# A gate table from fp32r products with high and low gates, its one-hots from two digits, and six Gelus behind the gates' exponent

## The reference

```python
def chunk_fn(xc):
    q = (xc @ w_query).reshape(C, PEER_HEADS, 2, PEER_HALF)
    sc = jnp.einsum('thpd,hpnd->thpn', q, sub_keys)
    top_s, top_i = lax.top_k(sc, 16)
    ...
    best_s, best_pos = lax.top_k(cand_s, 16)
    experts = jnp.take_along_axis(cand_i, best_pos, axis=-1)   # i1 * 128 + i2
    gates = jax.nn.softmax(best_s, axis=-1)
    u, vv = expert_down[experts], expert_up[experts]
    act = gelu(jnp.einsum('cd,chkd->chk', xc, u))
    return jnp.einsum('chk,chkd->cd', gates * act, vv)
```

## Time and profile before

| | |
|---|---|
| median of 3 runs | 1761.45 us (1759.91 to 1761.52) |
| profiled execution, its own time | 1758.45 us |
| its span, first to last instruction | 1756.3 us |
| mean granted TensorE clock | 0.963 of full |
| TensorE busy | 1594.7 us |
| VectorE busy | 1078.8 us |
| ScalarE busy | 712.9 us |

### The profile page before, as it was taken

The page is one execution under the profiler, slowest core; times in us unless marked ns, Lnnn a source line. Parts: engine busy times, 40 slices in busy tenths (PEclk is TensorE's granted clock), DMA queues, the critical chain, the costliest instruction groups (busy, mean ns, idle before and its releaser), DMA issues. The chain is left out here.

```text
span 1756.3 us, 29202 instructions
## 1 busy us (share of the span) xinstructions
PE 1594.7 (91%) x9001; PEld 1408.5 (80%) x9001; DVE 1078.8 (61%) x2744; ACT 712.9 (41%) x1526; POOL 5.1 (0%) x11
## 2 busy tenths in 40 slices
PE   2997699999998999999999999699999998778897
PEld 1664488879997888999999999589999997568785
DVE  2577457948996776666666666555455554257664
ACT  1333211113323444444444444365555554345552
POOL 0000000000000000000000000000000000000000
PEclk9998799999999999999999999799999999689998
DMA  6310133432224555555555555465555552065510
GB/s 257 145 37 1 44 131 119 151 131 85 91 91 168 192 193 191 185 184 191 190 185 186 183 188 191 173 205 144 147 147 147 138 129 53 1 206 158 160 30 24
DMA packets 151066, 244.50 MB, mean 139 GB/s; under 512 B 24144, under 2 KB 79952, under 8 KB 149968
## 3 DMA queue, kind: packets, MB, share of 16 engines
q1 hardware_dynamic: 150640, 243.51, 43.9%
q10 hardware_dynamic: 352, 0.07, 0.0%
HBM read 242.33 MB, written 1.20 MB: 139 GB/s over the span
## 5 line engine op out<-in xcount | busy, mean ns | idle before, releaser
L184 PE MATMUL experts_acc<-experts_uh,experts_wh 128*128 128x512 f32 x512 | 201.5, 394 | 5.6 <-DVE experts_ul L1546 5.6
L185 PE MATMUL experts_acc<-experts_ul,experts_wh 128*128 128x512 f32 x512 | 201.1, 393 | 0.0
L186 PE MATMUL experts_acc<-experts_uh,experts_wl 128*128 128x512 f32 x512 | 200.1, 391 | 0.0
L1099 PE MATMUL plain_u<-ffn_h,down_raw 128*128 128x256 f32 x832 | 192.2, 382 | 0.4 <-PEq L1184 0.4
L1519 ACT ACTIVATE experts_uh<-ffn_h 128x512 fp32r<-128x512 f32 x256 | 147.2, 623 | 83.7 <-PE experts_acc L186 79.0
L186 PE MATMUL projection<-hT_high,down_low 128*128 128x256 f32 x608 | 172.1, 283 | 0.0
L185 PE MATMUL projection<-hT_low,down_high 128*128 128x256 f32 x608 | 172.0, 283 | 0.0
L184 PE MATMUL projection<-hT_high,down_high 128*128 128x256 f32 x608 | 171.7, 282 | 0.0
L1099 PEld LDWEIGHTS plain_u<-ffn_h,down_raw 128*128 128x128 f32 x832 | 154.1, 192 | 19.5 <-issue 1.1
L1546 DVE TENSOR_TENSOR experts_ul<-ffn_h,experts_uh 128x512 fp32r<-128x512 f32 x256 | 164.8, 684 | 3.0 <-ACT experts_uh L1519 2.8
L184 PE MATMUL mix_a_pj<-mix_a_wh,hT_high 128*128 128x384 f32 x384 | 137.5, 358 | 18.2 <-DVE mix_a_wl L546 18.2
(11 more groups left out here) (270 smaller groups left out, 3083.5 us busy)
## 6 DMA issues: line engine op xcount, KB each, us to landing
down_raw<-in_downT SPq DMA_DIRECT2D x256, 256.0 KB, 3.5
ffn_h<-in_up SPq DMA_DIRECT2D x256, 256.0 KB, 2.8
mix_a_w_raw<-in_wa SPq DMA_DIRECT2D x48, 768.0 KB, 6.2
block_w_raw<-in_w SPq DMA_DIRECT2D x16, 768.0 KB, 6.3
mix_b_w_raw<-in_wb SPq DMA_DIRECT2D x16, 768.0 KB, 6.6
route_raw<-in_route SPq DMA_DIRECT2D x16, 576.0 KB, 3.8
bias_a<-bias_rows SPq DMA_DIRECT2D x16, 576.0 KB, 7.5
wo<-in_wo SPq DMA_DIRECT2D x2, 2048.0 KB, 10.3
```

The lines of the kernel that those rows point to most:

```text
L184: pe.matmul(out, lhs[0], rhs[0], start=start, stop=False, skip_group_check=True)
L185: pe.matmul(out, lhs[0], rhs[1], start=False, stop=False, skip_group_check=True)
L186: return pe.matmul(out, lhs[1], rhs[0], start=False, stop=stop, skip_group_check=True)
L1099: mm = pe.matmul(self.u[b][:, 0:SEQ], self.raw[b][:, k, :], self.h[:, k, :], start=k == 0, stop=k == KD - 1, skip_group_check=True)
```

## The change

1. EARLY goes from 28 to 24 and LATE from 24 to 28: four chunks are projected in `spread_phase` instead of `route_phase`. There TensorE takes 8 + 3 steps ahead of the first group (LEAD) and 3.375 per group afterwards, and a chunk is joined two groups behind its last step instead of one.
2. ScalarE computes the gates' exponent behind the 18th Gelu, and the last six Gelus after it.
3. VectorE finds the second index first. It splits the first index into a coarse digit (0 to 15) and a fine one (0 to 7), in four more operations on 128x256. Four arrays are turned and copied instead of three.
4. `a1` has a high part and a low part, both fp32r, and TensorE makes two fp32r products per token instead of one f32 product. The one-hots of the digits are made for eight groups at a time (`digits`), the coarse ones times the high gate; `a1h` is one product of the two per group on VectorE. ScalarE makes `a1l` from `a1h` by four activations per group whose scale is the ratio of low to high gate (`a1_low`), and does this for group g+1 before it evicts group g.

```diff
-EARLY = 28
-LATE = 24
+EARLY = 24
+LATE = 28
+BEFORE_GATE = 18
+LEAD = 8
+FINE = 8
...
-            for n, src in enumerate((index[0], index[1], gate)):
+            for n, src in enumerate((index[1], coarse, fine, gate)):
...
-            over_chunks(act, 0, EARLY, lambda n, b: plain.gelu(act, n, b, early[:, n, :]))
+            def early_gelu(n, b):
+                plain.gelu(act, n, b, early[:, n, :])
+            over_chunks(act, 0, BEFORE_GATE, early_gelu)
             act.wait_ge(shifted_ready, 1)
             act.activation(gate[:], shifted[:], ACT.Exp).then_inc(gate_exp, 1)
+            over_chunks(act, BEFORE_GATE, EARLY, early_gelu)
...
-            for half in range(2):
+            for half in (1, 0):
...
+            dve.tensor_scalar(eighth[:], index[0][:], 1.0 / FINE, -0.5 + 0.5 / FINE, ALU.mult, ALU.add)
+            dve.drain()
+            dve.tensor_scalar(eighth[:], eighth[:], WHOLE, None, ALU.add)
+            dve.drain()
+            dve.tensor_scalar(coarse[:], eighth[:], -WHOLE, None, ALU.add).then_inc(cols_ready, 1)
+            dve.drain()
+            dve.scalar_tensor_tensor(fine[:], coarse[:], -float(FINE), index[0][:], ALU.mult, ALU.add).then_inc(cols_ready, 1)
...
+    def steps_by(g):
+        return LEAD + (STEPS - LEAD) * (g + 1) // GROUPS if g >= 0 else 0
+    joins = [min(next(g for g in range(GROUPS) if steps_by(g) >= (n + 1) * KD) + 2, GROUPS) for n in range(LATE)]
...
+            def digits(n):
+                t = slice(n * BATCH * Q, (n + 1) * BATCH * Q)
+                for of, digit, base in ((coarse_of, "coarse", COARSE), (fine_of, "fine", FINE)):
+                    dve.tensor_tensor(of[:], iota[:, 0:base].unsqueeze(1).broadcast_to([P, BATCH * Q, base]),
+                                      slotT[digit][:, t].unsqueeze(2).broadcast_to([P, BATCH * Q, base]), ALU.is_equal)
+                dve.drain()
+                dve.tensor_tensor(coarse_of[:], coarse_of[:],
+                                  gate_h[:, t].bitcast(F32).unsqueeze(2).broadcast_to([P, BATCH * Q, COARSE]), ALU.mult)
+                dve.drain()
...
             def onehots(g):
                 b = g % 2
+                if g % BATCH == 0:
+                    digits(g // BATCH)
+                q = slice(g % BATCH * Q, g % BATCH * Q + Q)
                 wait(dve, g_ready, g - 1)
-                for q in range(Q):
-                    col = slice(g * Q + q, g * Q + q + 1)
-                    last = dve.tensor_scalar(a1[b][:, q, :], iota[:], slotT["i1"][:, col], slotT["gate"][:, col],
-                                             ALU.is_equal, ALU.mult)
-                last.then_inc(a1_ready, 1)
+                dve.tensor_tensor(a1h[b][:].rearrange("p q (h l) -> p q h l", l=FINE),
+                                  coarse_of[:, q].unsqueeze(3).broadcast_to([P, Q, COARSE, FINE]),
+                                  fine_of[:, q].unsqueeze(2).broadcast_to([P, Q, COARSE, FINE]), ALU.mult).then_inc(a1_ready, 1)
...
+            dve.tensor_copy(gate_h[:], slotT["gate"][:])
+            dve.drain()
+            dve.tensor_tensor(ratio[:], slotT["gate"][:], gate_h[:].bitcast(F32), ALU.subtract)
+            dve.tensor_scalar(floor[:], gate_h[:].bitcast(F32), TINY, None, ALU.max)
+            dve.drain()
+            dve.reciprocal(floor[:], floor[:])
+            dve.drain()
+            dve.tensor_tensor(ratio[:], ratio[:], floor[:], ALU.mult).then_inc(ratio_ready, 1)
...
                 for q in range(Q):
-                    mm = pe.matmul(gp[g % BANKS][:, q, :], a2[g % 2][:, q, :], a1[g % 2][:, q, :], start=True, stop=True)
+                    if q == 0:
+                        pe.wait_ge(a1l_ready, g + 1)
+                    pe.matmul(gp[g % BANKS][:, q, :], a2[g % 2][:, q, :], a1h[g % 2][:, q, :], start=True, stop=False,
+                              skip_group_check=True)
+                    mm = pe.matmul(gp[g % BANKS][:, q, :], a2[g % 2][:, q, :], a1l[g % 2][:, q, :], start=False, stop=True,
+                                   skip_group_check=True)
...
+            def a1_low(g):
+                act.wait_ge(a1_ready, g + 1)
+                wait(act, g_ready, g - 1)
+                for q in range(Q):
+                    last = act.activation(a1l[g % 2][:, q, :], a1h[g % 2][:, q, :].bitcast(F32), ACT.Copy,
+                                          scale=ratio[:, g * Q + q:g * Q + q + 1])
+                last.then_inc(a1l_ready, 1)
+            act.wait_ge(ratio_ready, 1)
+            a1_low(0)
             for g in range(GROUPS):
+                if g + 1 < GROUPS:
+                    a1_low(g + 1)
                 act.wait_ge(g_ready, g + 1)
```

More of the change, by code:

```diff
@@ L55 @@
 SKEW = 384
+WHOLE = 1.5 * float(1 << 23)
+TINY = 1e-30
 ROOT_SEED = float(0x5F3759DF - 0x00400000 - (1 << 30))
@@ L1210, in route_phase @@
         index = [sb(f"index{h}", [P, NT, SLOTS]) for h in range(2)]
+        eighth, coarse, fine = [sb(n, [P, NT, SLOTS]) for n in ("eighth", "coarse", "fine")]
         qp = [ps(f"qp{b}", [P, 512]) for b in range(2)]
@@ L1313, in _ @@
             dve.drain()
-            dve.tensor_scalar(part[:], pos[:], 4, None, ALU.logical_shift_right).then_inc(shifted_ready, 1)
+            dve.tensor_scalar(part[:], pos[:], TOPK - 1, None, ALU.bitwise_and).then_inc(shifted_ready, 1)
             dve.drain()
-            for half in range(2):
-                if half == 1:
-                    dve.tensor_scalar(part[:], pos[:], TOPK - 1, None, ALU.bitwise_and)
+            for half in (1, 0):
+                if half == 0:
+                    dve.tensor_scalar(part[:], pos[:], 4, None, ALU.logical_shift_right)
                     dve.drain()
@@ L1331, in _ @@
                     last = dve.tensor_reduce(index[half][:, t, :], picked[:], AX.X, ALU.add)
-                    if t == NT - 1:
+                    if half == 1 and t == NT - 1:
                         last.then_inc(cols_ready, 1)
                     dve.drain()
+            dve.tensor_scalar(eighth[:], index[0][:], 1.0 / FINE, -0.5 + 0.5 / FINE, ALU.mult, ALU.add)
[5 more added lines that the diff above has]
+            dve.scalar_tensor_tensor(fine[:], coarse[:], -float(FINE), index[0][:], ALU.mult, ALU.add).then_inc(cols_ready, 1)
             dve.wait_ge(gate_exp, 1)
@@ L1354, in spread_phase @@
     BANKS = 4
-    joins = [min(((n + 1) * KD * GROUPS + STEPS - 1) // STEPS + 1, GROUPS) for n in range(LATE)]
+    COARSE = P // FINE
+    BATCH = 8
+    def steps_by(g):
+        return LEAD + (STEPS - LEAD) * (g + 1) // GROUPS if g >= 0 else 0
+    joins = [min(next(g for g in range(GROUPS) if steps_by(g) >= (n + 1) * KD) + 2, GROUPS) for n in range(LATE)]
     def merged_rows(g):
@@ L1363, in sem, with sb @@
             return c.enter_context(nc.semaphore(f"spread_{n}"))
[L1365 to L1368, removed]
+        def sb(n, s, dt=F32):
+            return c.enter_context(nc.sbuf_tensor(f"spread_{n}", s, dt))
+        slotT = {k: sb(k, [P, SEQ]) for k in ("i2", "coarse", "fine", "gate")}
+        gate_h = sb("gate_h", [P, SEQ], F32R)
+        ratio, floor = sb("ratio", [P, SEQ]), sb("floor", [P, SEQ])
+        coarse_of, fine_of = sb("coarse_of", [P, BATCH * Q, COARSE]), sb("fine_of", [P, BATCH * Q, FINE])
+        a1h, a1l, a2 = [[sb(f"{n}{b}", [P, Q, P], F32R) for b in range(2)] for n in ("a1h", "a1l", "a2_")]
         before = [sb(f"before{b}", [P, SEQ]) for b in range(2)]
         gp = [c.enter_context(nc.psum_tensor(f"spread_g{b}", [P, Q, P], F32)) for b in range(BANKS)]
-        a1_ready, a2_ready, g_ready, g_kept, merged, joined = [sem(n) for n in ("a1", "a2", "g", "kept", "merged", "joined")]
+        a1_ready, a1l_ready, a2_ready, g_ready, g_kept, merged, joined, ratio_ready = [
+            sem(n) for n in ("a1", "a1l", "a2", "g", "kept", "merged", "joined", "ratio")]
         block = c.enter_context(nc.Block())
@@ L1419, in _ @@
             for g in range(GROUPS):
-                for m in range(STEPS * g // GROUPS, STEPS * (g + 1) // GROUPS):
+                for m in range(steps_by(g - 1), steps_by(g)):
                     n = EARLY + m // KD
```

2 lines of the change are left out of this document (1 added, 1 removed).

## The result

The changed kernel takes **1802.33 us** (median of 4 runs, 1799.1 to 1803.65) against 1760.68 us for the kernel before on the same chip (1759.83 to 1761.52): ratio **1.0234**, interval 1.0216 to 1.0252. The profiled execution took 1802.32 us, its span is 1800.3 us. Three views show where the time went.

The account below looks back on a forecast made before the run. TensorE set the pace before; the change makes a ring of 2.67 us per group the bound. Spread phase 202.2 against 145.5 us, +56.7, less 17.3 for the earlier start: +39.4, 1797.8 us profiled, 1801 median; range 1772 to 1818.

Parts of the forecast that it names:

- The ring: Spread phase: low-part activations, evictions, VectorE's merge and next one-hots wait on each other once per group, 2.67 us; chance 0.74.
- rounds with a join: Spread phase: each of 26 joins lies in the ring and adds 0.31 us to its round.
- a round with digits: Spread phase: making digits once in eight groups adds 1.86 us to that round, seven times.
- The activations: ScalarE's four low-part activations per group start 0.29 us apart, 1.17 us together, between bounds of 0.16 and 0.39.
- The products: TensorE in the spread phase: eight fp32r records per group at 0.110 us each, so no gain over f32.
- The 0.085 us a group for going from f32 back to fp32r: TensorE in the spread phase: this switch costs 0.26 instead of 0.17 us, once a group, making its work 2.43 us.
- the rivals at 1773 and 1739: Spread phase: activations 0.16 us apart, 1773, chance 0.09; fp32r records at 0.057 us and ring not binding, 1739, 0.06.
- The route's stall and the earlier start: End of route: four chunks moved (13.8 us) and the stall gone (3.5) start the spread phase 17.3 us sooner, at 373.7.
- Reciprocal: VectorE at the start of the spread phase: a reciprocal of 256 elements takes 1.9 us.
- the clock at the start, 3 us: First two groups of the spread phase: about six microseconds of half clock on TensorE cost 3 us, between nothing and 4.
- the median: Whole kernel: the profiled execution lies 3.0 us below the median of the runs, so 1797.8 becomes 1801 us.

Follow-up runs that it names:

- const_scale: Changed kernel with a constant scale instead of the column of ratios in the four low-part activations (low gates wrong): 1779.42 us, ratio 1.0108.
- no_low_product: Changed kernel without TensorE's four low-gate products per group, low parts still made and waited for: 1801.35 us, ratio 1.0235.
- three_buffers: Changed kernel with a third one-hot buffer and VectorE making one-hots of g+1 before merging g-1, all work kept: 1763.72 us, ratio 1.0021.
- low_64_columns: three_buffers with the low product on 64 of its 128 columns: 1765.66 us, ratio 1.0030.
- f32_three_buffers: Changed kernel with one f32 product per token, digit one-hots with the full gate, no low parts, and three buffers: 1755.79 us, ratio 0.9968.
- gelu_first: Changed kernel with the due late-chunk Gelu moved ahead of a1_low(g+1) on ScalarE: 1798.93 us, ratio 1.0233.

## Why the prediction was right, and what was off

**The ring** was right in kind and size. Turn 2.66 us measured, 2.67 predicted; rounds with a join 2.9 to 3.1, 2.98 predicted; a round with digits 4.53, 4.53 predicted (427.92 to 432.45 us below). const_scale, no_low_product and three_buffers together show it: a link shortened gives its whole length back, half of TensorE's products taken away leaves the turn as it is, the ring opened gives nearly all. Before the change nothing on ScalarE waited for VectorE's one-hots.

**The activations** start 0.298 us apart (four in 1.28) and last 0.38 to 0.39; 0.29 was taken between bounds of 0.16 and 0.39. With the constant scale of const_scale they start 0.20 apart and last 0.30 on average (four take 0.91), so the column costs 0.09 of length and 0.10 of distance. The formula of the Trainium skill ("ScalarE: Activation LUTs", What ACT_TABLE_LOAD costs) gave 386 and 293 ns, and this trace agrees (390 on average, 298 apart).

**The products** cost 0.111 us a record against 0.110 taken, so single-pass products bring TensorE nothing: eight records stay eight. low_64_columns shows that columns do not matter here, 64 or 128. The 0.085 us a group for going from f32 back to fp32r was wrong: the second record of a group does start 0.24 us behind the first, but the group is no longer for it. TensorE's records of three_buffers, where it sets the pace:

```profile
460.31 0.41 PE L1478 MATMUL spread_g<-spread_a1h,spread_a 128*128 128x128 f32 x1
460.55 0.28 PE L1480 MATMUL spread_g<-spread_a1l,spread_a 128*128 128x128 f32 x1
...
462.50 0.41 PE L1478 MATMUL spread_g<-spread_a1h,spread_a 128*128 128x128 f32 x1
```

A group of three steps takes 2.19 us with fp32r products here, 2.18 with f32 ones in f32_three_buffers (458.19 to 460.37 us), and one of four steps 2.62 in both. So TensorE's work was 2.35 us a group and not 2.43: nothing to the ring of 2.66, but 5 us too much in every sum in which TensorE sets the pace (the rivals at 1773 and 1739, and the expectation for three_buffers, whose 165 to 168 would have been 160 to 163, so that its measured 164.0 is not below the sum but 1 to 4 us above it).

Of the two figures of the Trainium skill ("TensorE: Matmul & The Clock Gate") the 107 ns for a load of weights stands beside the measured 0.111; the 81 ns per pair is not reached with this type.

**The route's stall and the earlier start**: 374.08 us measured, 373.7 predicted; the Exp and its changes of tables are hidden. Reciprocal 1.75 us against 1.9; last `a1_low` to the end 3.96 against 4.0; start to `a1_low(1)` 8.65 against 8.6.

**Off: the clock at the start, 3 us.** The phase took 206.1 us against 202.2 in the sum. From `a1_low(1)` to `a1_low(63)` are 193.5 us; rounds, joins and digits were 186.6. So 6.9 us stood where 3 had been counted, and most of it elsewhere than at the start. The timeline of the changed kernel at one batch of digits:

```profile
427.92 1.28 ACT L1499 ACTIVATE spread_a1l<-spread_a1h,spread_ratio 128x128 fp32r<-128x128 f32 x4 [0.95 <-DVE spread_a1h L1425]
...
432.45 1.28 ACT L1499 ACTIVATE spread_a1l<-spread_a1h,spread_ratio 128x128 fp32r<-128x128 f32 x4 [2.82 <-DVE spread_a1h L1425]
...
434.16 0.33 ACT L1492 ACTIVATE early<-plain_u 128x192 f32<-128x192 f32 x1
...
434.64 1.19 PE L1104 MATMUL plain_u<-ffn_h,down_raw 128*128 128x256 f32 x2 [3.30 <-ACT early L1492]
...
437.23 2.87 PE L1104 MATMUL plain_u<-ffn_h,down_raw 128*128 128x256 f32 x6
```

`a1_low` is late by the digits, the evictions and the Gelu stand behind it, and TensorE needs that Gelu's bank: it idles 3.30 us. Then six of its records take 2.87 us, where six at 444.00 us take 1.51, and the granted clock of these windows is 0.82 and 0.83. The prediction had TensorE idle for long only at the start and had its projections free of the ring; the 3 us were the term that was too small, 6.9 measured. gelu_first takes these waits away, and its phase of 198.7 us is the prediction's sum without its 3 us for the clock, 199.2. Half clock is left in it too (0.92 in 400 to 570 us, 0.93 in the changed kernel), so the waits, more than the clock, are what lengthened the phase. The 7.4 us rest on one trace of each kernel; the totals do not tell the two apart.

**Off, the other way: the median.** The sum gave 1797.8 us for a profiled execution; it was 1802.3, short by 4.5: 3.9 of it in the phase. To come to the median I had added the 3.0 us by which the profiled execution of before lay below its median. The one after lay on its median. The forecast of 1801 is as close as it is because these two partly cancel.

## What to carry to other kernels

Before new work is given to an engine that looks half idle, write down for one iteration who waits for whom in each engine's program order: a ring closed once per iteration costs the sum of its links, however idle each engine is (here 2.66 us with no engine over 86%). A shorter link gives back its length (22.9 and 32.7 of 41.7 us here), but only another order with one more buffer gave back nearly all with all work kept (38.6), and only then does a saving on the busiest engine count. Products whose weights change with each of them cost 0.11 us a record here, f32 or fp32r, 64 or 128 columns: only fewer records would make them cheaper, and two fp32r ones replace the two of one f32 product. The cheapest part of a change may be its best: putting one ScalarE operation, with its changes of tables, into idle time ahead gave 5.6 us of 1760 between the medians (ratio 0.9960, 0.9946 to 0.9974).

## What the runs showed of the hardware that I had not expected

- Tables are changed again and again. With the Exp moved ahead, ScalarE's later loop of Gelus loads a table before every second Gelu, where the kernel before loads none until the Exp. ScalarE in the changed kernel:

```profile
355.75 1.28 ACT L1115 ACT_TABLE_LOAD   x1 [1.32 <-PE plain_u L1104]
...
362.66 1.28 ACT L1115 ACT_TABLE_LOAD   x1 [3.06 <-PE plain_u L1104]
```

The prediction counted two changes. The further ones lie in ScalarE's idle time and cost nothing here; by my estimate from these rows a loop in which ScalarE is the bound would pay 1.28 us for each.

- Stages that no edit touches move by microseconds. In 160 to 240 us the granted clock was 0.70 to 0.77 in the traces, and the spread phase of kernels with the same split began up to 5 us apart. The clock of that window goes with it only in part: no_low_product had 0.74 and began at 374.6 us, const_scale had 0.77 and began at 376.3, and 2.4 us of gelu_first's 5.0 are from before it. A difference of that size between two totals is read from the phase before it is ascribed to an edit.
- Going from f32 to fp32r records and back costs TensorE nothing in a whole group (2.19 against 2.18 us), although the first distance is 0.24 instead of 0.11 us.
- A reciprocal of 256 elements per partition takes 1.75 us on VectorE, where a copy of the same size takes 0.42 us, so it is priced by its own row.
